# Holding V seven tiles instead of eight, signalling each tile's sum, and keeping twelve weight pieces in place of eleven

## The reference

```
u = expert_u[it]; vv = expert_v[it]                    # 128 picks a token
act = gelu(einsum('thkd,td->thk', u, xt))              # one dot product a pick
out = einsum('thk,thkd->td', gt * act, vv)             # weighted sum of the v rows
```

## Time and profile before

| | us |
|---|---|
| median of three runs | 2868.9 |
| profiled execution, its own time | 2871.69 |
| span in the profile, first to last instruction | 2869.8 |
| TensorE busy | 2214.0 (77%) |
| VectorE busy | 1976.9 (69%) |
| GpSimd busy | 1102.7 (38%) |
| ScalarE busy | 1085.8 (38%) |

### The profile page before, as it was taken

How to read it: one execution, slowest core, us unless ns; L and a number is a source line. 1 busy time by engine, 2 the same in 40 slices (tenths; PEclk the granted TensorE clock), 3 DMA queues, 4 the chain that set the end, 5 groups by cost and what they waited for, 6 DMA issues and landing times.

```text
span 2869.8 us, 29800 instructions
## 1 busy us (share of the span) xinstructions
PE 2214.0 (77%) x9194; PEld 1013.5 (35%) x9194; DVE 1976.9 (69%) x4743; ACT 1085.8 (38%) x3147; POOL 1102.7 (38%) x1037
## 2 busy tenths in 40 slices
PE   9788989778977999888887676677698655565555
PEld 6535625333532355344443232332254111111111
DVE  3757766787667586689756777887766666666654
ACT  2333423562334333386323544552233322222222
POOL 0223423343434433344334444443343444434342
PEclk9999999889998999999999889898899778777777
DMA  9999999999999999999999999999999999999998
GB/s 390 346 417 405 395 419 416 420 415 410 400 421 413 420 386 420 401 404 373 415 420 421 401 421 418 420 418 419 415 413 421 419 419 418 420 419 415 415 419 367
DMA packets 176558, 1175.48 MB, mean 410 GB/s; under 512 B 19600, under 2 KB 21264, under 8 KB 45328
## 3 DMA queue, kind: packets, MB, share of 16 engines
q0 software_dynamic: 147456, 1073.81, 90.7%
q1 hardware_dynamic: 28944, 99.78, 8.8%
HBM read 1169.31 MB, written 4.19 MB: 409 GB/s over the span
## 4 chain that ended last, share of the span: by engine, by line
DMA 35%; DVE 9%; PE 8%; issue 4%; ACT 3%; POOL 0%; POOLq 0%; ACTq 0%; DVEq 0%
DMA ring<-table_uv,idx_t 35%; DVE ring L1636 6%; PE acc L1054 4%; ACT wmask L1225 1%; PE pt L786 1%; PE pz L777 1%; POOL ring L763 0%; DVE rc L1293 0%; PE pt L777 0%; DVE hT L1293 0%; PE po L989 0%; PE po L786 0%; ACT dots L1220 0%; PE pz L962 0%; PE pt L772 0%
## 5 line engine op out<-in xcount | busy, mean ns | idle before, releaser
L1636 DVE CUSTOM_DVE_ANT_0 ring<-ring,h2r 128x1024 f32<-128x1024 f32 x1024 | 1246.7, 1222 | 780.2 <-DMA ring<-table_uv,idx_t 771.9
L763 POOL DMA_INDIRECT ring<-table_uv,idx_t x1024 | 1100.8, 1075 | 1749.4 <-DVE dots L1636 1094.1
L1054 PE MATMUL acc<-ring,wmask 128*64 128x512 f32 x4096 | 1185.7, 706 | 560.5 <-ACT wmask L1225 559.5
L1054 PEld LDWEIGHTS acc<-ring,wmask 128*64 128x64 f32 x4096 | 285.3, 152 | 1256.4 <-ACT wmask L1225 826.2
L1220 ACT ACTIVATE dots<-dots 128x2 f32<-128x2 f32 x512 | 104.0, 203 | 1517.4 <-DVE dots L1636 1503.1
L1225 ACT ACTIVATE wmask<-gmask,dots 128x64 f32<-128x64 f32 x1024 | 300.5, 340 | 48.3 <-ACT dots L1220 1.1
L1213 ACT ACTIVATE gmask<-stack,gate_t 128x64 f32<-128x64 f32 x1024 | 293.1, 334 | 0.6 <-DVE gate_t L1623 0.5
L786 PE MATMUL pt<-hT,w_held 128*128 128x256 f32 (+1 forms) x480 | 96.0, 349 | 0.0
L1220 ACT ACT_TABLE_LOAD x69 | 88.5, 1283 | 1.2
L786 PEld LDWEIGHTS pt<-hT,w_held 128*128 128x128 f32 x480 | 76.7, 197 | 25.4 <-issue 19.4
L989 PE MATMUL po<-rd,vals_sb 128*64 128x128 f32 x576 | 75.7, 303 | 12.0 <-ACT rd L1159 11.8
(11 more groups left out here) (315 smaller groups left out, 2236.0 us busy)
## 6 DMA issues: line engine op xcount, KB each, us to landing
w_ring<-wstream SPq DMA_DIRECT2D x103, 512.0 KB
ring<-wstream SPq DMA_DIRECT2D x32, 512.0 KB, 12.0
ring<-table_uv,idx_t POOLq DMA_INDIRECT x1024
w_held<-wstream SPq DMA_DIRECT2D x9, 512.0 KB, 13.6
xs<-x_in_dram SPq DMA_DIRECT2D x8, 512.0 KB
h2r<-wstream SPq DMA_DIRECT2D x8, 512.0 KB
scores<-wstream SPq DMA_DIRECT2D x8, 512.0 KB, 14.0
xs<-wstream SPq DMA_DIRECT2D x4, 512.0 KB, 11.9
```

What stands on the lines that cost most here:

```text
L763: nc.gpsimd.indirect_dma_start(out=ring[:, cell(t):cell(t) + 2, :].rearrange("p c d -> p (c d)"), out_offset=None, in_=table, in_offset=ba ...
L1054: mm = nc.tensor.matmul(acc[HALF * i:HALF * i + HALF, half * 512:(half + 1) * 512], wmask[:, slot, :], ring[:, cell(2 * p + i) + 1, half * ...
L1636: V.tensor_tensor_reduce(u, u, h2r[:, b % H_SLOTS, i, :], 1.0, 0.0, ALU.mult, ALU.add, dots[:, t % SLOTS:t % SLOTS + 1]).then_inc(dots_don ...
```

## The change

`V_HOLD` becomes 7. The ring then has 13 cells, and `cell(t)` turns over 12 tiles instead of 13. `pair_done` is replaced by `tile_summed`, which TensorE raises once for each tile; the matmuls of a pair are issued tile by tile (both halves of tile 2p, then both of 2p+1), where they were issued half by half. GpSimd waits for `tile_summed` of tile t-7. `HELD` becomes 12, in the room of the cell that goes. All names that are derived from these follow: `FIRST_HELD` 36, `FIRST_ROOM` 30.

```diff
--- before.py
+++ after.py
@@ -29,7 +29,7 @@
 QUARTERS = 4
 QPICKS = PICKS // QUARTERS
 SLOTS = 8
-U_HOLD, V_HOLD = 5, SLOTS
+U_HOLD, V_HOLD = 5, 7
 TURN = U_HOLD + V_HOLD
 CELLS = TURN + 1
 W_SLOTS = 3
@@ -39,7 +39,7 @@
 S_SLOTS = 7
 MIX_LAG = 3
 PIECES = 48
-HELD = 11
+HELD = 12
 LENT = 2
 EARLY = 32
 SPARE = 5
@@ -544,7 +544,7 @@
         gmask_ready = sem("gmask_ready")
         gelu_done = sem("gelu_done")
         wmask_ready = sem("wmask_ready")
-        pair_done = sem("pair_done")
+        tile_summed = sem("tile_summed")
         acc_free = sem("acc_free")
         x_free = sem("x_free")
         half_summed = sem("half_summed")
@@ -757,7 +757,7 @@
                     pool.wait_ge(soon_kept, 1)
                 elif t == 2 * SOON or t and t % QPICKS == 0:
                     pool.wait_ge(idx_kept, nth(b, q))
-                wait(pool, pair_done, (t - V_HOLD) // 2 + 1)
+                wait(pool, tile_summed, t - V_HOLD + 1)
                 if cell(t) + 2 < CELLS:
                     wait(pool, dots_done, t - U_HOLD + 1)
                 nc.gpsimd.indirect_dma_start(
@@ -1048,16 +1048,16 @@
                     mm = nc.tensor.matmul(acc[:, cols], ident[:], xs[:, p // PAIRS % X_SLOTS, cols], start=True, stop=False)
                     if half:
                         mm.then_inc(x_free, 1)
-                for half in range(2):
-                    for i in range(2):
+                for i in range(2):
+                    for half in range(2):
                         slot = (2 * p + i) % SLOTS
                         mm = nc.tensor.matmul(acc[HALF * i:HALF * i + HALF, half * 512:(half + 1) * 512],
                                               wmask[:, slot, :],
                                               ring[:, cell(2 * p + i) + 1, half * 512:(half + 1) * 512],
                                               start=False, stop=(p % PAIRS == PAIRS - 1))
-                    if p == BLOCKS * PAIRS - 1 and half == 0:
-                        mm.then_inc(half_summed, 1)
-                mm.then_inc(pair_done, 1)
+                        if p == BLOCKS * PAIRS - 1 and i == 1 and half == 0:
+                            mm.then_inc(half_summed, 1)
+                    mm.then_inc(tile_summed, 1)
 
             pe.wait_ge(ident_set, 1)
             pe.wait_ge(ones_set, 1)
@@ -1229,7 +1229,7 @@
             def finish(b):
                 cols = slice(0, D if b < BLOCKS - 1 else 512)
                 if b < BLOCKS - 1:
-                    act.wait_ge(pair_done, (b + 1) * PAIRS)
+                    act.wait_ge(tile_summed, (b + 1) * PICKS)
                 else:
                     act.wait_ge(half_summed, 1)
                     act.wait_ge(y_out[b % 2], 16 * (b // 2))
@@ -1637,7 +1637,7 @@
                                        dots[:, t % SLOTS:t % SLOTS + 1]).then_inc(dots_done, 1)
 
             def finish_half(b):
-                dve.wait_ge(pair_done, (b + 1) * PAIRS)
+                dve.wait_ge(tile_summed, (b + 1) * PICKS)
                 dve.wait_ge(y_out[b % 2], 16 * (b // 2))
                 V.tensor_copy(staged(b)[:, 512:D], acc[:, 512:D]).then_inc(last_half, 1)
```

## The result

The changed kernel takes 2903.96 us, the median of four runs (2896.53 to 2914.87), against 2868.9 us before (2867.12 to 2869.51): a ratio of 1.0124, with a 95% interval of 1.0109 to 1.0139. In a later series of runs it was 1.0138 (1.0123 to 1.0154), 2908.1 against 2868.0 us. The forecast was 2894 us, range 2863 to 2936. The four runs of the changed kernel lie 18 us apart. The profiled execution took 2896.53 us, the lowest of those four; its span is 2894.6 us, 24.8 us above that of before.

A forecast was written before the change was run, and what follows sets the result against it. DMA engines bound the kernel: 2799 us of bytes at 420 GB/s plus 71 us with too little to do. Profiled 2871.7 + 30 - 5 = 2896.7 us, 2894 in the runs' terms; range 2863 to 2936.

The forecast's parts named there:

- The mechanism: GpSimd's tile issue: odd tiles wait one pair later, for the signal of the next even tile; both then issue together.
- 12 places x 2.49 = +30 us: Twelve stretches under 400 GB/s where TensorE is late or nearly so; each loses one tile's time, 2.49 us.
- cushion of 2.55 us: Tile issue to use: 10.30 us in the quiet end less 7.75 with a dry queue; later issue leaves DMA idle.
- one in four of the 117 waits: Upper bound: of GpSimd's waits for TensorE's sums between 100 and 1600 us, 29 cost a tile each, +72 us.
- Where it was to be lost: DMA rate falls between 250 and 1600 us at places where it already dips; nothing changes after 2100 us.
- The bytes, -5.0 us: Streamed weights in groups 1 to 4: four pieces, 2.10 MB, not read again, counted in full at 420 GB/s.
- The signal by tile gives nothing: On TensorE a pair's two tiles run side by side and end together, so `tile_summed` of tile 2p brings forward nothing.
- TensorE's work unchanged, rival B: A pair's sum stays 1.94 us, cost 0; rival B: overlap lost, 3.1 to 3.5 us a pair, about 3000 us, chance 0.09.
- The start, 0: At the start 13 and not 14 weight pieces are asked for at once; twelve ahead cover the landing, cost 0.
- The quiet end, 0: In the quiet end an odd tile goes 1.7 us later, under the cushion of 2.55, so cost 0.
- Rival A (hidden): Four tiles in flight cover the later issue, or weights fill the holes; only the bytes show, 2864 us; chance 0.20.
- C (faster): Streamed pieces and sums come sooner, half of 39 us of dips goes, no odd tile held up; about 2854, chance 0.07.

The follow-up runs named there:

- the run with 16 pieces: Kernel before, with the last four streamed pieces of each of groups 1 to 4 cut to 16 of 1024 columns; 2854.4 us against 2869.6, ratio 0.9956.
- the one with two: Kernel before, with streamed piece 36 cut to 16 of 1024 columns, which took effect only in groups 3 and 4; 2867.0 us, ratio 0.9997.

## Why the prediction was right, and where it was off

- **The mechanism.** Right. The later wait of the odd tiles by itself costs 46 us, more than the whole change, and nothing else was found that adds to it. It shows in the rows as was forecast: GpSimd's waits for TensorE up, for dots down, the long ones now before odd tiles (22 over 5 us, where 2 were), five DMAs of `w_ring` fewer.
- **The size of it: the term "12 places x 2.49 = +30 us".** This step was mis-sized, twice and in opposite directions. At the twelve places the loss is 17 us, 1.4 us a place, 0.6 of a tile's time. The boundary at 1204.96 us shows one way: of the 2.7 us that tile 392 lost on tile 390, 1.3 were back at tile 395; whether it is so at all twelve was not read. Elsewhere, counted at zero, it is 33 us. The forecast took a place for harmless if the DMA rate there stood above 400 GB/s before. A full rate tells that the queue was not empty, not how far it was from empty: with a cushion of 2.55 us, read from one tile on each side, and a delay of 2.5 us on average plus the 1.25 us between issues, many places without any dip can go over. That this is how the 33 us arise is argued, not shown. The upper bound, one in four of the 117 waits, looked at such places, but at 72 us was too high: the loss is 46 / 2.49 = 18 to 19 tiles' times, between the 12 and the 29. That the total came within 16 us of the term, and the forecast within 10 us of the result, is in part luck: two errors of 13 and 33 us stand against each other.
- **Where it was to be lost.** Partly. The forecast put it between 250 and 1600 us, where the rate dipped. Of the 25.5 us by which the last tile goes out later, 18.9 were lost by tile 512, and 7 more between it and tile 704; among the twelve places were just two behind tile 512. After 2100 us nothing more was lost, as forecast.
- **The bytes, -5.0 us.** Too large: about 3 us by the run with 16 pieces; the one with two can't tell. The term assumed that the queue is full wherever a piece is streamed. Pieces are streamed in just the stages that have the holes, which may be the reason; no run shows it.
- **The signal by tile gives nothing.** Right, in both rings. The records of the two tiles run side by side, with the last ones 13 ns apart, so the first tile's end is the pair's.
- **TensorE's work unchanged, rival B.** Right to set it aside: a pair's eight records still take 1.94 us. By the rule of the Trainium skill in "TensorE: Matmul & The Clock Gate", Part 2, that matmuls stay in program order, a run of four in one half of the columns would have cost 3.1 us a pair; the row at 1507.16 us does not agree with it.
- **The start, 0.** Right within a microsecond. GpSimd's first tile goes out at 91.51 us in the changed kernel, and before at 90.8. The half microsecond or so seems to go with the twelfth piece and not with the ring: the other profiles with 13 cells and 12 pieces lie at 91.6 to 91.7, that with 13 cells and 11 pieces at 91.0, and those with 14 cells and 11 pieces at 90.8 to 91.0. Of the changed kernel:

```profile
91.51 1.09 POOL L763 DMA_INDIRECT ring<-table_uv,idx_t  x1 [88.61 <-DVE idx_t L1350]
```

- **The quiet end, 0.** Right: 418 GB/s in both. From 2300 to 2800 us GpSimd's waits for TensorE rose from 37 (56.5 us, longest 2.6) to 54 (119.6 us, longest 6.3), and no tile was lost by them: tile 768 goes out 25.1 us later than before, the last one 25.5.
- **Rival A (hidden) and C (faster).** Both fell. No run shows the 10 us that C expected from dips that get less; the ninth tile, another means to that end, brought 3 to 4 us.

The sum of the parts as measured: +46 for the wait, -3 for the bytes, 0 for the rest, 43 us, against 35 and 40 us in the two series of the changed kernel. The 3 to 8 us between them are near the noise between series; the ring of 13 cells with 11 pieces, which by this sum should cost 46, costs 42 to 43. Nothing here settles whether the difference is real.

## What to carry to other kernels

When a buffer is recycled by a signal that covers several tiles, write down for each tile which signal it waits for before and after. Here one tile less of V moved only the odd tiles' wait, but by a whole pair. Measure the cushion (issue to use with a full queue, less the same with an empty one) and compare it with the distribution of the new delays, not with the places that starve already. And don't take a saved byte at its full price where the queue has holes: here it brought 0.6 of that. After an experiment that leaves something out, look at the bytes of its page: one of those here left out half of what it was meant to.

## What the runs showed that was not expected

- The curve is steep on one side and flat on the other: one tile less of V costs 46 us, one more gives 4 us, with four more pieces to load in it (about 3 us). Of GpSimd's two waits, that for the sums is the larger with seven tiles (841 us to 674), that for the dots with eight (1094 to 469) and more so with nine (1244 to 348), so a sum that comes still earlier finds the other wait ahead of it.
- GpSimd's indirect DMAs got longer: 1128 ns on average in the changed kernel, 1075 before, 54 us in all. 243 of them take over 1.2 us, where 162 did; of those issued right behind another it is 30%, of the rest 20% (before 21% and 14%). Some of each kind:

```profile
111.19 1.72 POOL L763 DMA_INDIRECT ring<-table_uv,idx_t  x1 [4.18 <-DVE dots L1636]
113.21 0.94 POOL L763 DMA_INDIRECT ring<-table_uv,idx_t  x1 [0.30 <-issue]
...
136.39 0.94 POOL L763 DMA_INDIRECT ring<-table_uv,idx_t  x1 [3.00 <-DVE dots L1636]
137.63 1.97 POOL L763 DMA_INDIRECT ring<-table_uv,idx_t  x1 [0.30 <-issue]
```

  What makes them long was not tried. The kernel with the later wait alone has 237 of them, so they come with the wait.
- In groups of matmuls whose outputs lie in different halves of the columns, a run of four records of one half overlapped with the four of the other. So it was for the values in the earlier trace rows (16 records in 1.15 us, where one behind the other would be 1.76), and for the sums by tile in the changed kernel and in the old ring (eight in 1.94 us, where it would be 3.5).
- Some of the kernels with the later wait spread more from run to run: 2897 to 2915 us for the changed one, 2898 to 2922 for that with the pair signal, where the kernel before stays within 2862 to 2874. But the kernel with that wait alone stays within 2915 to 2921 over five runs, so the wait by itself doesn't explain it.
